# Second block's norm factor applied to the products' results instead of their operand; chunk 0's products placed behind chunk 1's tiles

## The chip, the cores and the metric

One core of one Trainium2 chip runs the kernel. The metric is the device time of one execution in microseconds (us). Engines are named as in the profile: PE (TensorE matmul), PEld (its weight loads), DVE (VectorE), ACT (ScalarE), POOL (GpSimd) and SP (SyncE, which issues the loads).

## The reference, cut to what matters

T = 256 tokens, D = 2048, all in float32. Two blocks run one after the other. The first is an adaLN-modulated neighbourhood attention and a convolutional feed-forward; the second a hybrid layer with an mLSTM and a latent attention, whose input products all come from one normed operand:

```python
def rms_norm_2(x, g):
    x32 = x.astype(jnp.float32)
    y = x32 * lax.rsqrt(jnp.mean(x32 * x32, axis=-1, keepdims=True) + EPS)
    return (y * g.astype(jnp.float32)).astype(x.dtype)
...
    h = rms_norm_2(x, norm_g)
    proj = jnp.einsum('bsd,dn->bsn', h, w_in)
...
    (q_a, k_a, v_a, o_a, i_a, f_a, z_a, c_q, c_kv, k_r, z_b, g_a, g_b) = jnp.split(proj, offsets, axis=-1)
    qk_a = jax.nn.silu(causal_depthwise_conv(jnp.concatenate([q_a, k_a], axis=-1), conv_w))
```

The factor `rsqrt(mean(x*x) + EPS)` is one number per token. It can multiply the operand `h`, or every result of `h @ w_in`, since the product is linear in each token's row. What follows each result differs: `c_q` and `c_kv` are normed again, `k_r` gets its rotation, `i_a` and `f_a` get a bias, `q_a` and `k_a` go through a four-tap convolution along the tokens, `v_a` goes into the mLSTM as it is, and the others pass a sigmoid or silu.

## The kernel before

**Products.** A product is computed in full precision from two parts of each operand: a high part and the rest. A weight tile of 128 x 1024 floats (512 KB) is loaded into one of five buffers `raw`; ACT makes its high part `wh` (L1179), DVE the rest `wl` (L1576), always two tiles ahead of PE (three buffers each). The operand's parts lie in XHL, FHL, HHL and so on. PE does three matmuls per piece: high by high, high by rest, rest by high. Products whose result has tokens in the partitions use L935 to L937 or L926 to L928 (these three with 512 columns); the result lies in PG, a pair of PSUM areas used in turn.

**The order of the work.** `Program` (L156) writes one list of steps by hand: a step is one slice of a product (half a weight tile as a rule), a tile of the adaLN product, or idle. `schedule()` (L258) hangs pieces of other work on steps: `P.put(where, plus, job, key, phase)` places a phase of a job `plus` steps behind a place. Every engine walks the same list and does its own part of each step, in this order: the split of the tile two ahead, the step's matmuls, the side work. So an engine that waits in one piece holds up all that stands behind it on that engine. SP issues the loads in the order of `plan`.

**The start.** The adaLN product comes in eight chunks of eight tiles (L831). While they load, the products for k and v of the first group are done too, two weight tiles per chunk: `early(c)` (L847 to L862), which needs the rows of the shift and scale of chunk c turned into columns (`rows`, L955 and L963 on PE, AR on ACT) and the operand modulated with them (`mod`: MT on DVE, XHL on ACT). In the plan chunk 1 stands as two tiles, two weight tiles, six tiles; the other chunks as eight tiles with the two weight tiles of the chunk before behind them. `early(0)` stands behind the fourth tile of chunk 1, every other behind the eighth tile of its next chunk.

**Attention of the first block.** Heads go in groups of two (g, with hh = 0 and 1). Ten phases of a head stand at steps counted from a place given by hand in `schedule()` (L307 to L312): scores, softmax (SB), its transpose (PT, L1287 on ACT), the product with VB (L1040 on PE) and OHL.

**The border.** The last product of the first block is down1 (four groups). Each group's result is added to the residual XT (`residual`: L1824, L1825, L1828 on DVE). `normed` hangs the second block's norm behind it: ACT squares the last quarter of XT (L1206), DVE makes the factor xr (L1694 to L1604, twelve small operations one after the other), ACT (L1212) and DVE (L1705) multiply XT by it into HNH, PE transposes HNH in eight sets of four (`turned`, L1104; the first three sets ahead of the first product lat 0), and ACT and DVE make the parts of HHL, with the norm's weight g. Behind the last matmul of down1 PE does 28 matmuls whose result nobody reads (`warm`, L1013).

**The second block.** Its products are lat (q and kv latents), small (rotary key and gates), mqk and mv (mLSTM, four groups each, in turn), then sig, silu, out, mix and mixb with others. What follows each: ACT squares of lat (L1352) and LTMP (L1358); small: ACT copies KRF out of PSUM (L1329), DVE adds the biases to the gates (L1895, L1897), PE takes KRF (L1047). Group g of mqk is convolved while mv g is computed (`m_conv`): ACT multiplies the result by the last tap into MQK (L1368, the centre), DVE adds the three others (L1943, three for each of the four quarters, at steps 1 to 4 of mv g) and ACT applies silu. Head 2g + 1 of the mLSTM runs beside mv g + 1: ACT and DVE make ME and MA (L1958) from the gates and scores, DVE multiplies them into MP (L1967), and PE takes MP at L1075.

## Time and profile before

| | |
|---|---|
| median of 3 runs | 2552.49 us (2551.92 to 2555.49) |
| the profiled execution | 2552.33 us, span 2550.3 us, mean granted clock 0.998 |
| PE busy | 2511.5 us, 98% of the span |
| DVE busy | 1619.7 us, 64% |
| ACT busy | 1251.4 us, 49% |
| POOL busy | 143.7 us, 6% |
| DMA | 511.42 MB, 201 GB/s over the span |
| chain that ended last | PE 94%, ACT 2%, DVE 2%, SP's queue 1% |

The span is the time from the first to the last recorded instruction; the execution's own time has about 2 us more around it. A row of a timeline gives the start, the busy time, the engine, the line of the kernel, what is written from what, and in brackets the idle time of the engine before it with what ended it. PEclk is the granted clock of TensorE as a share of full speed (1.00 is 2.4 GHz, 0.50 is 1.2 GHz). Of a busy share, what counts is whether PE, the engine that is hardly ever idle, waits for that engine.

### The profile page before, as it was taken

Reading aid. Unit: us, or ns where it says so; the run is one execution under the profiler, and the core shown is the slowest. Engines: PE = TensorE matmul, PEld = TensorE weight load, DVE = VectorE, ACT = ScalarE, POOL = GpSimd, SP = SyncE. Lnnn points to the kernel's source line nnn. Section 1 sums busy time; section 2 is a strip of 40 time slices with the busy share of each in tenths; the row PEclk is TensorE's granted clock in tenths of the full one; section 3 lists DMA queues with packets and bytes.
Section 4 is the critical chain, followed back from the end, with each engine's and each line's share of the span. In section 5 each row is a group of like instructions: output and inputs, shape, how many; then the busy total and the mean of one; then the engine's idle time right before and its main releaser. Section 6 shows DMA issues by size and latency. Waiting matters only on the chain.

```text
span 2550.3 us, 34507 instructions
## 1 busy us (share of the span) xinstructions
PE 2511.5 (98%) x13608; PEld 2131.9 (84%) x13608; DVE 1619.7 (64%) x2365; ACT 1251.4 (49%) x1899; POOL 143.7 (6%) x148
## 2 busy tenths in 40 slices
...
GB/s 335 333 182 112 233 245 249 244 240 183 206 193 273 266 261 191 193 189 189 191 189 192 163 169 174 174 170 184 174 164 150 157 166 189 181 190 183 189 189 165
DMA packets 459104, 511.42 MB, mean 201 GB/s; under 512 B 36771, under 2 KB 327682, under 8 KB 458432
## 3 DMA queue, kind: packets, MB, share of 16 engines
...
q8 instruction: 107, 1.75, 0.3%
q14 instruction: 53, 0.43, 0.1%
q10 hardware_dynamic: 144, 0.02, 0.0%
...
## 4 chain that ended last, share of the span: by engine, by line
PE 94%; ACT 2%; DVE 2%; SPq 1%; issue 1%; DMA 0%; DVEq 0%; ACTq 0%
PE PG L926 17%; PE PG L928 17%; PE PG L927 17%; PE PG L916 13%; PE PG L919 6%; PE PG L935 4%; PE PG L937 4%; PE PG L936 4%; PE PS L1040 1%; SPq L746 1%; PE PS L831 1%; ACT wh L1179 1%; PE PG L847 1%; PE PS L1104 1%; PE PG L849 1%
## 5 line engine op out<-in xcount | busy, mean ns | idle before, releaser
L1576 DVE TENSOR_TENSOR wl<-raw,wh 128x1024 fp32r<-128x1024 f32 (+1 forms) x745 | 911.3, 1227 | 702.7 <-ACT wh L1179 701.0
L1179 ACT ACTIVATE wh<-raw 128x1024 fp32r<-128x1024 f32 (+1 forms) x745 | 786.7, 1058 | 860.7 <-PE PG L928 574.8
L916 PE MATMUL PG<-FHL,wh 128*128 128x512 f32 x1376 | 430.8, 396 | 2.4 <-DVE UP L1832 1.5
L926 PE MATMUL PG<-wh,HHL 128*128 128x512 f32 x832 | 331.2, 398 | 0.1
L928 PE MATMUL PG<-wl,HHL 128*128 128x512 f32 x832 | 324.8, 390 | 0.0
L927 PE MATMUL PG<-wh,HHL 128*128 128x512 f32 x832 | 324.1, 390 | 0.0
L919 PEld LDWEIGHTS PG<-FHL,wl 128*128 128x128 f32 x1376 | 256.2, 188 | 59.6
L919 PE MATMUL PG<-FHL,wl 128*128 128x256 f32 x1376 | 267.9, 278 | 0.0
L916 PEld LDWEIGHTS PG<-FHL,wh 128*128 128x128 f32 x1376 | 210.8, 189 | 5.2 <-issue 3.7
L928 PEld LDWEIGHTS PG<-wl,HHL 128*128 128x128 f32 x832 | 156.1, 188 | 33.6
L927 PEld LDWEIGHTS PG<-wh,HHL 128*128 128x128 f32 x832 | 156.5, 188 | 30.7
L926 PEld LDWEIGHTS PG<-wh,HHL 128*128 128x128 f32 x832 | 156.3, 188 | 30.6 <-DVE HHL L2069 0.4
L1562 DVE SCALAR_TENSOR_TENSOR ada_acc<-raw,CSs,ada_acc 128x1024 f32<-128x1024 f32 x120 | 161.7, 1347 | 4.7 <-DMA raw<-in_w_ada 0.6
L935 PE MATMUL PG<-XHL,wh 128*128 128x256 f32 (+1 forms) x448 | 150.5, 336 | 0.0
L937 PE MATMUL PG<-XHL,wl 128*128 128x256 f32 (+1 forms) x448 | 147.3, 329 | 0.0
L936 PE MATMUL PG<-XHL,wh 128*128 128x256 f32 (+1 forms) x448 | 147.3, 329 | 0.0
L927 PE MATMUL PG<-wh,HID 128*128 128x512 f32 x344 | 133.8, 389 | 0.0
L926 PE MATMUL PG<-wh,HID 128*128 128x512 f32 x344 | 133.8, 389 | 0.0
L928 PE MATMUL PG<-wl,HID 128*128 128x512 f32 x344 | 133.8, 389 | 0.0
L926 PE MATMUL PG<-wh,XHL 128*128 128x256 f32 x384 | 110.6, 288 | 0.0
L928 PE MATMUL PG<-wl,XHL 128*128 128x256 f32 x384 | 108.6, 283 | 0.0
L927 PE MATMUL PG<-wh,XHL 128*128 128x256 f32 x384 | 108.6, 283 | 0.0
...
## 6 DMA issues: line engine op xcount, KB each, us to landing
...
raw<-in_w_ada SPq DMA_DIRECT2D x128, 512.0 KB, 5.0
...
```

The source lines that it names most:

```text
L746: sp.dma_start(dst[:, :, col:col + wd], src).then_inc(s_raw[P.slot[i]], 16)
L916: pe.matmul(to, hi[:, 128 * j:128 * j + 128], flat(FHL[:, step.k, :, :]), start=step.first, stop=False, skip_group_check=True)
L919: end = pe.matmul(to[:, 0:T], lo[:, 128 * j:128 * j + 128], xh, start=False, stop=step.last, skip_group_check=True)
L926: pe.matmul(dst, xh[:, cols], hi, start=step.first and j % per == 0, stop=False, skip_group_check=True)
L927: pe.matmul(dst, xl[:, cols], hi, start=False, stop=False, skip_group_check=True)
L928: end = pe.matmul(dst, xh[:, cols], lo, start=False, stop=step.last, skip_group_check=True)
L935: pe.matmul(dst, hi[:, c0:c1], xh, start=step.first and j % per == 0, stop=False, skip_group_check=True)
L936: pe.matmul(dst, hi[:, c0:c1], xl, start=False, stop=False, skip_group_check=True)
L937: end = pe.matmul(dst, lo[:, c0:c1], xh, start=False, stop=step.last, skip_group_check=True)
L1179: ac.activation(wh[n % NSPL][:, 0:src.shape[1]], src, ACT.Copy).then_inc(S["hi"], 1)
L1562: dv.scalar_tensor_tensor(out=acc[:, :], in0=raw_of(i), scalar=CSs[:, 0, k:k + 1], in1=acc[:, :], op0=ALU.mult, op1=ALU.add).then_inc(S["a ...
L1576: dv.tensor_tensor(wl[n % NSPL][:, 0:x], src, wh[n % NSPL][:, 0:x], ALU.subtract).then_inc(S["lo"], 1)
```

## The change

It has three parts.

1. *Start.* In the plan every chunk stands as five adaLN tiles, the two weight tiles of the chunk before, three tiles. `early(0)` stands behind all eight tiles of chunk 1, and the rows of chunk 1 are turned at `early(0)` instead of at chunk 1's last tile.
2. *Attention, g = 1.* Phases 6 to 9 of head 2 move from steps 25, 25, 26, 26 to 27, 27, 29, 29, and those of head 3 by up to two steps.
3. *The second block's norm.* XT is transposed as it is: six of the eight sets during down1, two during lat 0. `warm` and the products HNH are gone. The factor is made during lat 0. Where tokens lie in the partitions, ACT multiplies by xr in the operation it does anyway, in two halves instead of one (lat, mv, sig, silu, out, mix, mixb). Where they lie in the columns, the factor is needed as a row: DVE makes DIAGH (identity times xr), PE multiplies it by ones into all partitions (new L1027), ACT copies that to RR. DVE then multiplies small's results by RR and adds the biases after it, and multiplies the whole result of mqk by RR into a new tile MSG, from which centre and taps read. The file's lines move: L926 to L928 are L936 to L938, L1576 is L1598, L1179 is L1195, L1104 is L1120, L1075 is L1089.

```diff
-            tiles, n = chunk_tiles(c), 2 if c == 1 else 8
+            tiles, n = chunk_tiles(c), 5
...
-                if c and n % 8 == (3 if c == 1 else 7):
+                if c and n % 8 == 7:
...
-        at = ("early", c - 1, 0) if c > 1 else ("chunk", 8 * c + 7, 0)
+        at = ("early", c - 1, 0) if c else ("chunk", 8 * c + 7, 0)
...
-            after, plus = ("k", 2, 0), ((14, 15, 16, 17, 18, 19, 25, 25, 26, 26), (27, 27, 28, 28, 29, 30, 32, 32, 33, 34))
+            after, plus = ("k", 2, 0), ((14, 15, 16, 17, 18, 19, 27, 27, 29, 29), (27, 28, 29, 29, 30, 31, 33, 33, 34, 35))
...
     residual("down1", ("tail2", 0, 0), 0, "h")
-    normed("h", ("tail2", 0, 0), ("lat", 0, 0))
+    P.put(("lat", 0, 0), 1, "norm", "h", 0)
+    for phase, n in enumerate((2, 4, 5)):
+        P.put(("lat", 0, 0), n, "rows_h", 0, phase, phase == 1)
+    for i in range(8):
+        turned("xh", i, ("down1", i // 2 + 1, 0) if i < 6 else ("lat", 0, 0), (5 if i < 6 else 3) + 3 * (i % 2))
...
+        P.put(("mv", g, 0), 0, "m_conv", g, 6)
         P.put(("mv", g, 0), 0, "m_conv", g, 0)
...
-             "xf": (HN["f"], FHL[:, :, :, :].rearrange("p k a t -> p a k t"), "f", A1[:, 0, :]), "xh": (HN["h"], HHL, "h", g2)}
+             "xf": (HN["f"], FHL[:, :, :, :].rearrange("p k a t -> p a k t"), "f", A1[:, 0, :]), "xh": (XT, HHL, "h", g2)}
...
-                p = P.of["up" if key == "f" else "lat", 0]
+                p = P.of["up", 0]
                 t = p + 1
...
+            elif (job, phase) == ("rows_h", 1):
+                w.wait_ge(S["diag_h"], 1)
+                w.wait_ge(*free(u))
+                pe.matmul(ps[:, 0:T], ones[:, :], flat(DIAGH[:, :, :]), start=True, stop=True).then_inc(S["side"], 1)
...
-            elif (job, phase) == ("small", 0):
-                w.wait_ge(*product_done("small", 0))
-                ac.activation(KRF[:, :], result("small", 0)[0:64, 0, 0:T], ACT.Copy).then_inc(S["kr_raw"], 1)
+            elif (job, phase) == ("rows_h", 2):
+                u = use("rows_h", 0, 1)
+                w.wait_ge(*full(u))
+                ac.activation(RR[:, :], bank(u)[:, 0:T], ACT.Copy).then_inc(emptying(u), 1)
...
                 w.wait_ge(*product_done("lat", key))
+                w.wait_ge(S["xr"], 2)
                 if key == 1:
                     w.wait_ge(S["lat_r"], 1)
                 for n in range(2):
-                    end = ac.activation(LJUNK[:, n, :], result("lat", key)[:, n, :], ACT.Square,
+                    end = ac.activation(LJUNK[:, n, :], result("lat", key)[:, n, :], ACT.Square, scale=xr[:, n:n + 1],
...
                 g, b = key, key % 2
-                w.wait_ge(*product_done("mqk", g))
+                w.wait_ge(*out_done("mqk", g))
                 if g >= 2:
                     w.wait_ge(*full(use("mlstm", 2 * g - 3, 0, 1)))
                 for j in range(4):
                     ch = 8 * (j // 2) + 2 * g + j % 2
-                    end = ac.activation(MQK[b][:, j, :], result("mqk", g)[:, j // 2, T * (j % 2):T * (j % 2) + T],
-                                        ACT.Identity, scale=cw2[:, 3, ch:ch + 1])
+                    end = ac.activation(MQK[b][:, j, :], MSG[b][:, j, :], ACT.Identity, scale=cw2[:, 3, ch:ch + 1])
                 end.then_inc(S["m_centre"], 1)
...
-                ac.activation(RG[n % 2][:, :, :], result(name, g)[:, :, :],
-                              ACT.Sigmoid if name == "sig" else ACT.Silu).then_inc(out_sem(name, g), 1)
+                for j in range(2):
+                    end = ac.activation(RG[n % 2][:, j, :], result(name, g)[:, j, :],
+                                        ACT.Sigmoid if name == "sig" else ACT.Silu, scale=xr[:, j:j + 1])
...
                 ps = result("small", 0)
-                dv.tensor_scalar(gates[:, 0, :], ps[64:72, 0, 0:T], gb[:, 0:1], None, ALU.add)
-                w.wait_ge(S["kr_raw"], 1)
-                dv.tensor_scalar(gates[:, 1, :], ps[96:104, 0, 0:T], gb[:, 1:2], None,
-                                 ALU.add).then_inc(out_sem("small", 0), 1)
+                w.wait_ge(*product_done("small", 0))
+                w.wait_ge(*emptied(use("rows_h", 0, 1)))
+                dv.tensor_tensor(KRF[:, :], ps[0:64, 0, 0:T], RR[0:64, :], ALU.mult).then_inc(S["kr_raw"], 1)
+                dv.tensor_tensor(gates[:, 0, :], ps[64:72, 0, 0:T], RR[64:72, :], ALU.mult)
+                dv.tensor_tensor(gates[:, 1, :], ps[96:104, 0, 0:T], RR[96:104, :], ALU.mult).then_inc(c.sem, c.up())
+                w.wait_ge(c.sem, c.n)
+                dv.tensor_scalar(gates[:, 0, :], gates[:, 0, :], gb[:, 0:1], None, ALU.add)
+                dv.tensor_scalar(gates[:, 1, :], gates[:, 1, :], gb[:, 1:2], None, ALU.add).then_inc(out_sem("small", 0), 1)
+            elif (job, phase) == ("rows_h", 0):
+                w.wait_ge(S["xr"], 2)
+                dv.tensor_tensor(DIAGH[:, :, :], ident[:, :].unsqueeze(1).to_broadcast([128, 2, 128]),
+                                 xr[:, :].unsqueeze(2).to_broadcast([128, 2, 128]), ALU.mult).then_inc(S["diag_h"], 1)
+            elif (job, phase) == ("m_conv", 6):
+                g, b = key, key % 2
+                w.wait_ge(*product_done("mqk", g))
+                w.wait_ge(*emptied(use("rows_h", 0, 1)))
+                if g >= 2:
+                    w.wait_ge(S["m_centre"], g - 1)
+                dv.tensor_tensor(MSG[b][:, :, :], result("mqk", g)[:, :, :].rearrange("p a (c n) -> p (a c) n", c=2),
+                                 RR[:, :].unsqueeze(1).to_broadcast([128, 4, T]), ALU.mult).then_inc(out_sem("mqk", g), 1)
...
-                dv.tensor_copy(lr[:, 2 * key:2 * key + 2], y).then_inc(S["lat_r"], 1)
+                dv.tensor_tensor(lr[:, 2 * key:2 * key + 2], y, xr[:, :], ALU.mult).then_inc(S["lat_r"], 1)
...
                 w.wait_ge(S["m_centre"], g + 1)
+                w.wait_ge(*out_done("mqk", g))
                 for k in (2, 1, 0):
                     d = 3 - k
                     end = dv.scalar_tensor_tensor(
-                        out=MQK[b][:, j, d:T], in0=result("mqk", g)[:, j // 2, T * (j % 2):T * (j % 2) + T - d],
+                        out=MQK[b][:, j, d:T], in0=MSG[b][:, j, 0:T - d],
                         scalar=cw2[:, k, ch:ch + 1], in1=MQK[b][:, j, d:T], op0=ALU.mult, op1=ALU.add)
```

How DVE's order changes at mv 1, with head 1 beside it. wl is a weight tile's rest, MQK the convolution's sum, MA and MP belong to the head. Before:

```order
L1576 TENSOR_TENSOR wl_65<-raw_53,wh_62 128x1024
L1943 SCALAR_TENSOR_TENSOR MQK_187<-PG,cw_101,MQK_187 128x255
L1943 SCALAR_TENSOR_TENSOR MQK_187<-PG,cw_101,MQK_187 128x254
L1943 SCALAR_TENSOR_TENSOR MQK_187<-PG,cw_101,MQK_187 128x253
L1576 TENSOR_TENSOR wl_66<-raw_49,wh_63 128x1024
L1958 TENSOR_TENSOR MA<-PS,caus_k 128x256
L1943 SCALAR_TENSOR_TENSOR MQK_187<-PG,cw_101,MQK_187 128x255
```

Now:

```order
L1598 TENSOR_TENSOR wl_65<-raw_53,wh_62 128x1024
L1935 TENSOR_TENSOR MSG_217<-PG,RR 128x1024
L1982 SCALAR_TENSOR_TENSOR MQK_187<-MSG_217,cw_101,MQK_187 128x255
L1982 SCALAR_TENSOR_TENSOR MQK_187<-MSG_217,cw_101,MQK_187 128x254
L1982 SCALAR_TENSOR_TENSOR MQK_187<-MSG_217,cw_101,MQK_187 128x253
L1598 TENSOR_TENSOR wl_66<-raw_49,wh_63 128x1024
L1997 TENSOR_TENSOR MA<-PS,caus_k 128x256
L1982 SCALAR_TENSOR_TENSOR MQK_187<-MSG_217,cw_101,MQK_187 128x255
```

MSG has come in between the split of the third tile of mv 1 and the first tap; the rest is in its old order.

PE at the border, from the last matmuls of down1 (HID is its operand) to the first of lat 0 (HHL). Before:

```order
L927 MATMUL PG<-wh_62,HID 128x512
L928 MATMUL PG<-wl_65,HID 128x512
L1013 MATMUL PG<-wh_63 128x512 x28
L1104 MATMUL PS<-ident,HNH 128x128 x12
L926 MATMUL PG<-wh_63,HHL 128x512
L927 MATMUL PG<-wh_63,HHL 128x512
L928 MATMUL PG<-wl_66,HHL 128x512
```

Now, from the last piece of lat 0's second tile on; the two tiles ahead of it follow down1 with nothing between:

```order
L937 MATMUL PG<-wh_64,HHL 128x512
L938 MATMUL PG<-wl_67,HHL 128x512
L1120 MATMUL PS<-ident,XT 128x128 x4
L936 MATMUL PG<-wh_62,HHL 128x512
L937 MATMUL PG<-wh_62,HHL 128x512
L938 MATMUL PG<-wl_65,HHL 128x512
L936 MATMUL PG<-wh_62,HHL 128x512
L937 MATMUL PG<-wh_62,HHL 128x512
L938 MATMUL PG<-wl_65,HHL 128x512
L1027 MATMUL PS<-DIAGH,ones 128x256
L936 MATMUL PG<-wh_62,HHL 128x512
```

The filler and the twelve transposes that stood ahead of lat 0 are gone; one set of four transposes stands behind its second tile, and the matmul on DIAGH in the middle of its third.

DVE's order there, from the last residual of down1 to the second block's first operand parts. Now:

```order
L1847 TENSOR_TENSOR RTMP<-PG,G_166 128x512
L1850 TENSOR_TENSOR XT<-RTMP,XT 128x512 x2
L1598 TENSOR_TENSOR wl_65<-raw_51,wh_62 128x1024
L1716 SCALAR_TENSOR_TENSOR xss<-xsq,xss 128x2
...
L1626 SCALAR_TENSOR_TENSOR xr<-CV 128x2
L1598 TENSOR_TENSOR wl_66<-raw_52,wh_63 128x1024
L1927 TENSOR_TENSOR DIAGH<-ident,xr 128x256
L1598 TENSOR_TENSOR wl_67<-raw_53,wh_64 128x1024
L2120 SCALAR_TENSOR_TENSOR HHL<-PS,g_91,HHL 128x256 x2
```

Before, the norm followed the residual with no split between, and the split of the third tile stood behind six sets of transposes:

```order
L1825 TENSOR_TENSOR RTMP<-PG,G_166 128x512
L1828 TENSOR_TENSOR XT<-RTMP,XT 128x512 x2
L1694 SCALAR_TENSOR_TENSOR xss<-xsq,xss 128x2
...
L1604 SCALAR_TENSOR_TENSOR xr<-CV 128x2
L1705 TENSOR_SCALAR HNH<-XT,xr 128x256 x3
L2069 SCALAR_TENSOR_TENSOR HHL<-PS,g_91,HHL 128x256 x2
...
L1705 TENSOR_SCALAR HNH<-XT,xr 128x256
L1576 TENSOR_TENSOR wl_65<-raw_51,wh_62 128x1024
```

The split of lat 0's third tile has moved ahead of the norm chain, and DIAGH stands behind the chain and one more split.

## Rows read from the trace of the kernel before

**Rows 1.** The page, section 1: busy time and instructions of each engine.
```profile
PE 2511.5 (98%) x13608; PEld 2131.9 (84%) x13608; DVE 1619.7 (64%) x2365; ACT 1251.4 (49%) x1899; POOL 143.7 (6%) x148
```

**Rows 2.** Table by stage: stretch, its length, busy us (instructions) by engine, clock, DMA.
```profile
42.00:53.00 11.00, 11.00 (x48) 8.96 (x48) 0.00 (x0) 1.79 (x3) 0.00 (x0) 0.98 1.10 348
...
63.10:66.00 2.90, 2.84 (x7) 2.27 (x8) 1.14 (x2) 0.18 (x1) 0.00 (x0) 0.50 1.10 351
...
269.00:272.00 3.00, 0.54 (x5) 0.37 (x4) 2.05 (x3) 2.72 (x5) 0.00 (x0) 1.00 0.02 10
```

**Rows 3.** Timeline of PE, start: start us, us, engine, line, operands, [idle before].
```profile
39.94 1.92 PE L831 MATMUL PS<-raw,CSP 128*32 128x512 f32 x4
...
53.20 1.92 PE L831 MATMUL PS<-raw,CSP 128*32 128x512 f32 x16
...
63.16 0.80 PE L847 MATMUL PG<-XHL,wh 128*128 128x512 f32 x1 [2.67 <-DVE wl L1576]
...
76.66 0.64 PE L831 MATMUL PS<-raw,CSP 128*32 128x512 f32 x4
```

**Rows 4.** Timeline of ACT, start.
```profile
74.02 1.06 ACT L1179 ACTIVATE wh<-first 128x1024 fp32r<-128x1024 f32 x1 [1.52 <-DMA first<-in_w_qkv]
```

**Rows 5.** Timelines of ACT and PE, head work of g = 1.
```profile
270.76 1.07 ACT L1287 ACTIVATE PT<-PS 128x512 f32<-128x512 f32 x2
...
271.92 1.32 PE L1040 MATMUL PS<-PT,VB 128*128 128x256 f32 x5 [2.46 <-ACT PT L1287]
```

**Rows 6.** Timeline of PE, border between the two blocks.
```profile
1443.40 6.51 PE L1013 MATMUL PG<-wh 128*128 128x512 f32 x28
1450.75 1.53 PE L1104 MATMUL PS<-ident,HNH 128*128 128x128 f32 x12 [0.84 <-ACT HNH L1212]
1452.42 0.50 PE L926 MATMUL PG<-wh,HHL 128*128 128x512 f32 x1
```

**Rows 7.** Timelines of DVE and ACT, border between the two blocks.
```profile
1445.73 1.28 DVE L1828 TENSOR_TENSOR XT<-RTMP,XT 128x512 f32<-128x512 f32 x2
1447.82 0.16 DVE L1694 SCALAR_TENSOR_TENSOR xss<-xsq,xss 128x2 f32<-128x2 f32 x1 [0.80 <-ACT HNH L1206]
...
1450.19 1.31 ACT L1212 ACTIVATE HNH<-XT,xr 128x256 f32<-128x256 f32 x3 [2.40 <-DVE xr L1604]
```

**Rows 8.** Timeline of DVE, mv 1 with head 1 beside it.
```profile
1580.68 1.23 DVE L1576 TENSOR_TENSOR wl<-raw,wh 128x1024 fp32r<-128x1024 f32 x1 [1.66 <-ACT wh L1179]
1582.14 1.52 DVE L1943 SCALAR_TENSOR_TENSOR MQK<-PG,cw,MQK 128x255 f32<-128x255 f32 x3 [0.23 <-ACT MQK L1368]
1583.69 1.22 DVE L1576 TENSOR_TENSOR wl<-raw,wh 128x1024 fp32r<-128x1024 f32 x1
1584.83 0.42 DVE L1958 TENSOR_TENSOR MA<-PS,caus_k 128x256 f32<-128x256 f32 x1
...
1589.40 0.55 DVE L1967 SCALAR_TENSOR_TENSOR MP<-PS,ME 128x384 f32<-128x384 f32 x1
```

**Rows 9.** Timeline of PE, mv 1, where PE takes MP.
```profile
1590.01 0.70 PE L1075 MATMUL PS<-MV,MP 128*128 128x257 f32 x2
```

**Rows 10.** Groups of DVE instructions by line: busy us, mean ns, idle before.
```profile
L1716 DVE SCALAR_TENSOR_TENSOR MT<-X,A,RX 128x256 f32<-128x256 f32 x16 | 7.7, 482 | 0.9
...
L1943 DVE SCALAR_TENSOR_TENSOR MQK<-PG,cw,MQK 128x254 f32<-128x254 f32 x16 | 7.7, 481 | 0.6
...
L2021 DVE TENSOR_TENSOR QKT<-PG,CV 128x1024 f32<-128x1024 f32 x8 | 9.8, 1224 | 0.3
```

**Rows 11.** Timelines of DVE and PE, mv 0.
```profile
1540.73 1.22 DVE L1576 TENSOR_TENSOR wl<-raw,wh 128x1024 fp32r<-128x1024 f32 x1
...
1543.04 0.39 PE L926 MATMUL PG<-wh,HHL 128*128 128x512 f32 x1
```

**Rows 12.** Timelines of DVE and PE, small product.
```profile
1509.15 0.48 DVE L1895 TENSOR_SCALAR gates<-PG,gb 8x256 f32<-8x256 f32 x1
...
1508.96 0.33 PE L1047 MATMUL PS<-ident,KRF 64*128 64x64 f32 x2
```

More of the change, by code:

```diff
@@ L583, in build @@
     RT = at("RT", [128, 2, 4, 64], F32, 199)
+    DIAGH = at("DIAGH", [128, 2, 128], F32, 178)
+    RR = at("RR", [128, T], F32, 179)
+    MSG = [at(f"MSG{i}", [128, 4, T], F32, 140 + 4 * i) for i in range(2)]
     KRH = at("KRH", [128, 2, 4, 64], F32, 201)
@@ L608, in xready @@
         u = use("turned", ("x" + z, k // 2), 0)
-        return emptied(u + k) if k < 2 else emptied(u)
+        return emptied(u + k) if z == "f" and k < 2 else emptied(u)
     def bank(u):
@@ L1095, in piece @@
                 w.wait_ge(*free(u))
-                apart = name in ("xf", "xh") and i == 0
+                apart = name == "xf" and i == 0
                 for ch in range(2):
@@ L1377, in piece @@
                     w.wait_ge(*full(use("mlstm", 2 * key - 3, 4, 1)))
-                ac.activation(MV[key % 2][:, :, :, 0:T], result("mv", key)[:, :, :].rearrange("p j (h e) -> p j h e", h=2),
-                              ACT.Copy).then_inc(out_sem("mv", key), 1)
+                for n in range(2):
+                    end = ac.activation(MV[key % 2][:, n, :, 0:T], result("mv", key)[:, n, :].rearrange("p (h e) -> p h e", h=2),
+                                        ACT.Copy, scale=xr[:, n:n + 1])
+                end.then_inc(out_sem("mv", key), 1)
             elif (job, phase) == ("mlstm", 2):
@@ L1415, in piece @@
                     w.wait_ge(*full(use("turned", ("ha", 7), 0)))
-                ac.activation(cols4(GA if name == "mix" else GB, g), result(name, g)[:, :, :],
-                              ACT.Sigmoid).then_inc(out_sem(name, g), 1)
+                for j in range(2):
+                    end = ac.activation(cols4(GA if name == "mix" else GB, g)[:, j, :], result(name, g)[:, j, :],
+                                        ACT.Sigmoid, scale=xr[:, j:j + 1])
+                end.then_inc(out_sem(name, g), 1)
             elif (job, phase) == ("qr_out", 0):
@@ L1506, in piece @@
                 w.wait_ge(*full(u))
-                if name in ("xf", "xh") and i == 0:
-                    if name == "xf":
-                        w.wait_ge(S["gain"], NCH + 1)
+                if name == "xf" and i == 0:
+                    w.wait_ge(S["gain"], NCH + 1)
                     for k in range(2):
```

33 lines of the change are left out of this document (16 added, 17 removed).

## The prediction

> **What bounds the kernel now.** The page's first section was read first: PE is busy 2511.5 of 2550.3 us, DVE 64% and ACT 49% [rows 1]. So only PE's own instructions and its waits count; a change on DVE or ACT counts where PE waits for it. The table by stage then places the waits. The stretches of the start show DMA at a share of 1.10, PE at half clock (0.50) in 63.1 to 66, and a wait at 269 to 272 with the clock at 1.00 [rows 2]. Last came the timelines of PE, DVE and ACT at the places the change touches: the start [rows 3, 4], 271.92 [rows 5], the border between the blocks [rows 6, 7], the mLSTM heads [rows 8 to 10] and the small product [rows 12]. After 76 us no wait of PE is longer than 2.5 us. A gain must therefore come from PE instructions removed or from one of these few waits, and a delay costs only what exceeds the slack PE has there. About 0.2% (5.1 us) is what a measurement of this kernel can tell from no change.
>
> **Start (load plan, chunk 0's products behind chunk 1's tiles).** Loads set the pace. The 14th load is used at 39.94 [rows 3] and the 37th at 74.02 [rows 4], so one takes 34.08 / 23 = 1.48 us. The first 18 loads are the same set in another order, and chunk 1's last tile is the 18th: it lands at 39.94 + 4 x 1.48 = 45.9. Chunk 0's products began right behind the tiles of 39.94 (1.92 us) and ended at 53.20, 11.4 us later [rows 3]; now they begin near 47 and end near 59 (11.4 of their own, 0.8 for the L963 group that follows chunk 1's tiles). In return the 1.9 us of tiles that stood behind them at 53.20 are done before, and the 2.67 us wait at 63.16 for the weights of chunk 1's products should go, because those weights and chunk 1's modulated rows are made while chunk 0's products still run. Chunk 2's eight tiles (3.6, at 1.92 for four, less the overlap) then end near 63. Chunk 1's products took 63.16 to 76.66, 13.5 us, of which about 1.4 was half clock; without that they end near 75.2. That is 1.4 us earlier. Against it, PE does only short tile work with gaps before 47, and may begin chunk 0's products at half clock as it did at 63.16, which would return up to 1.4. I take **+1.0 us gained** (ends: -0.5 and +2.2). Once ahead, PE gives the next chunk's loads a little less time, but a chunk takes 3.6 + 12.0 = 15.6 us on PE at full clock and its ten loads 14.8, so 0.8 us is left each time.
>
> **Places of head work for g = 1.** The wait of 2.46 us at 271.92 is for ACT's PT copies, 270.76 to 271.8, which ACT does behind an operand split [rows 5]. PE's step moves from 26 to 29, about three steps later, so this wait goes. But ACT now has the VB eviction ahead of PT (128x1024 like a split's, so some 1.0 us, [rows 4]), and DVE and ACT have the next head's copies behind it, so two waits of about 1 us are what is late next. I take **+0.6** (ends -1 and +2.5).
>
> **Border between the blocks.** Before, from the last product of the first block at 1443.40 to the first of the second at 1452.42, PE does 28 filler matmuls (6.51), waits 0.84 and does 12 transposes (1.53) [rows 6]. Five later sets of four transposes add 0.35 each, so 9.02 + 1.75 = 10.8 us in all. Now eight sets of four (2.8) and one 128x256 matmul (0.45) remain: 7.5 us less. Two new waits take part of it. XT is final at 1447.0 (DVE L1828, from 1445.73), ACT's squares of it are done at 1447.8, where DVE's chain begins at 1447.82 [rows 7]. The second block's third weight tile is split behind these: ACT to 1448.8, DVE to 1450.0. PE, which starts at 1443.40 and spends 2.73 us on a tile, wants it at 1443.40 + 5.45 + 0.35 = 1449.2: a wait of 0.8. Behind that split stand the norm chain (2.4 us, 1447.82 to 1450.19 before), the fourth tile's split (1.2) and DIAGH (0.42), so DIAGH is ready at about 1453.9, while PE reaches its matmul at 1451.4: a wait of 2.5. Net 7.5 - 3.3 = **+4.2** (ends: +7.5 with no new wait, +2.5 if the clock falls after the second one).
>
> **mLSTM heads 1, 3, 5.** This is the term that decides. In mv 1 to mv 3, DVE has no idle time between the first tap at 1582.14 and MP, which ends at 1589.95; PE takes MP at 1590.01, with the sequencer there just in time [rows 8, 9]. The change puts MSG (128x1024 out of PSUM) into DVE's order between the wl split at 1580.68 and the first tap, and makes ACT's centre wait for it, where it ran beside that split before. An instruction follows a wl split after 1.14 us (1583.69 to 1584.83), so MSG starts at 1581.82; a 128x1024 multiply out of PSUM takes 1.22 [rows 10]; the centre starts at 1583.1. It reads SBUF now: four at the 0.40 us spacing of L1212 [rows 7] end at 1584.8. The taps start at 1584.85 instead of 1582.14, **2.7 us later**, and everything behind them is as before: wl, MA, six taps, wl, MP. Three times 2.7 = 8.1 us lost. In mv 0 there is no head, but the fifth tile's split, 1540.73 to 1541.95, moves by 2.7 to 1544.65, and PE wants it at 1543.04 [rows 11]: 1.6 more. **-9.7 in all.** The lower bound is zero only if PE had slack at 1590.01, which the rows exclude; 2.3 each (a centre as fast as from PSUM, a tap shorter) gives -8; a fall of the clock after such a wait adds 1.4 each.
>
> The taps read SBUF now. Rows show no gain in that: a tap out of PSUM takes 481 ns, the same operation all out of SBUF 482 [rows 10]. The Trainium skill (VectorE: DVE Perf Modes, "Rules for kernel authors" and the table of its section on the TRN2 errata) speaks for the copy: it advises moving a matmul result to SBUF before many operations on it, and its table has 62 cycles less for a source in SBUF. By that, an estimate from the page, each of nine taps would be 65 ns shorter and each of the three waits 0.6 us shorter; the row on L1716 does not bear it out.
>
> **Small product.** KRF is no longer an ACT copy but DVE's, behind two splits, where the first gate operation stood at 1509.15; it ends at 1509.6 and PE, which took it at 1508.96, waits 0.65 [rows 12]. Three more DVE operations follow, but ACT's gate chain starts late by the same 0.65, so the later wait near 1520 keeps its size. **-0.7** (ends 0 and -2).
>
> **Edits at about nothing.** HNH's scalings leave DVE and ACT at the border, where they were already counted. Evictions in two halves add about 0.25 us each on ACT; between them and the next PE wait ACT has idle time in the head stages, else they would cost up to 0.5 in all. I take -0.1. SP's loads are otherwise in the old order.
>
> **Sum:** 1.0 + 0.6 + 4.2 - 9.7 - 0.7 - 0.1 = -4.7, so 2552.3 (the profiled execution; the median of the runs, 2552.5, is 0.2 above it) becomes 2557.0, and as a median **2557.2 us**.
>
> **Rivals.** (1) *The clock falls after the new waits.* Four waits of 2.5 to 2.7 us are new. After the 2.67 us at 63.16 the next 2.9 us went at half clock, after the 2.46 us at 271.92 they did not [rows 2, 5]: the rows allow both. At two of four it costs 1.4 x 2 = 2.8, so 2560; at all four 2563. The filler matmuls that the change removes kept PE busy at the border. The Trainium skill (TensorE: Matmul & The Clock Gate, "Why this matters for your kernels") warns of idle gaps between bursts of matmuls, since they bring the array back to the low clock. Chance 0.25. (2) *The mLSTM stages absorb MSG.* If MP or its consumer had about 2.7 us of slack, the sum turns to +5.0 and with the border's gain whole to +8: 2544 to 2547. For it: DVE is only 64% busy. Against: the row at 1590.01 comes 0.06 after MP's end. It decides from about 0.5 us of slack per stage upward, and a full turn to faster needs all. Chance 0.12. (3) *The parts cancel.* The centre and taps cost 2.2 instead of 2.7, the border loses only one wait and the start gives its upper end: -6.6 - 1.1 (mv 0) + 6.5 + 2 + 0.6 - 0.8 = +0.6, so 2551.7; between this and the forecast lies 2552 to 2555. Chance 0.2. My forecast has 0.43.
>
> **Numbers.** The forecast's own spread, 2555 to 2559, straddles the border of 2557.6, so it gives half of its 0.43 to slower and half to no change. With rival 1 slower gets 0.21 + 0.25, rival 3 gives 0.2 to no change, rival 2 0.12 to faster. Slower 0.46, same 0.42, faster 0.12. The range leaves out rival 2 and rival 1 at all four places with more beside it: 2549 to 2564.
>
> **What the profile after would show.** Right: three waits of 2.3 to 2.7 us at the first PE instruction that takes MP (L1089 in the new file), a wait near 1.5 in mv 0 for a wl split, one near 2.5 for DIAGH at the new L1027 and one below 1 for wl before it; no filler matmuls at the second border; chunk 1's products beginning right behind chunk 2's tiles. Wrong: no wait for MP, which would mean that DVE was not the one on whom PE waited; PEclk under 1.00 behind the waits (rival 1); or chunk 0's products starting after 49.

## The result and the profile after

The changed kernel takes 2562.41 us (median of 6 runs, 2561.57 to 2563.57) where before takes 2552.41 (6 runs): **10.0 us slower**, ratio 1.0037 with a 95% interval of 1.0027 to 1.0048. The forecast was 2557.2 with a range of 2549 to 2564: right in its sign and its range, but 4.7 us of loss were forecast and 10.0 came, so half of the size.

The page of the kernel after, sections 1 and 4, beside [rows 1]:

```profile
span 2561.2 us, 34472 instructions
...
PE 2512.7 (98%) x13582; PEld 2129.4 (83%) x13582; DVE 1623.5 (63%) x2365; ACT 1253.0 (49%) x1915; POOL 143.4 (6%) x148
...
PE 92%; DVE 3%; ACT 2%; SPq 1%; issue 1%; DMA 1%; DVEq 0%; ACTq 0%
```

PE is busy 2512.7 us, 1.2 more than before although the filler is gone, and the span grew by 10.9 us: the rest is new waiting. DVE's share of the chain went from 2% to 3%. Now PE's waits of the kernel after (line waited at, who ended the wait, us in total, times, the longest):

```profile
...
PE PS L1089 <- DVE MP L2006: 7.6, 3, 2.6
PE PS L841 <- DMA raw<-in_w_ada: 3.2, 1, 3.2
PE PS L841 <- DMA first<-in_w_ada: 2.8, 3, 1.9
PE PS L1159 <- ACT LS L1503: 2.3, 3, 0.8
PE PS L1027 <- DVE DIAGH L1927: 2.2, 1, 2.2
PE PG L936 <- DVE wl L1598: 1.8, 2, 1.2
...
PE PS L1166 <- ACT LP L1510: 1.0, 3, 0.3
...
PE PS L1061 <- DVE KRF L1919: 0.5, 1, 0.5
```

L1089 takes MP (L1075 before), L1027 is the matmul on DIAGH, L936 waits for weight tiles' wl (in lat 0 and in mv 0), L1166 for LP in the latent attention. The waits at L1089, L1027, L936, L1166 and L1061 were not there before; the one at L1159 was 1.7 us in all.

Where the time went, by the start of the same matmul in the two traces:

| stretch | PE against before | forecast |
|---|---|---|
| start, up to 76 us | -1.8 | -1.0 |
| attention, g = 1 | -0.5 | -0.6 |
| 428 us (L993 waits for SQ) | +0.7 | none |
| border, down1 to the middle of lat 0 | -2.4 | -4.2 |
| small product (KRF) | +0.7 | +0.7 |
| mv 0 (wl) | +1.5 | +1.6 |
| mv 1, 2, 3: three waits for MP | +8.3 | +8.1 |
| half clock behind two of these three | +2.9 | none (rival 1) |
| latent attention (L1166) | +1.5 | +0.1 |
| sum | +10.9 | +4.7 |

The rows of the mLSTM stage, DVE in mv 1, the same instructions as in [rows 8]:

```profile
1579.04 1.23 DVE L1598 TENSOR_TENSOR wl<-raw,wh 128x1024 fp32r<-128x1024 f32 x1 [1.65 <-ACT wh L1195]
1580.19 1.22 DVE L1935 TENSOR_TENSOR MSG<-PG,RR 128x1024 f32<-128x1024 f32 x1
1583.18 1.52 DVE L1982 SCALAR_TENSOR_TENSOR MQK<-MSG,cw,MQK 128x255 f32<-128x255 f32 x3 [1.78 <-ACT MQK L1386]
1584.73 1.23 DVE L1598 TENSOR_TENSOR wl<-raw,wh 128x1024 fp32r<-128x1024 f32 x1
1585.88 0.42 DVE L1997 TENSOR_TENSOR MA<-PS,caus_k 128x256 f32<-128x256 f32 x1
...
1590.46 0.55 DVE L2006 SCALAR_TENSOR_TENSOR MP<-PS,ME 128x384 f32<-128x384 f32 x1
```

ACT's centre, four instructions, and PE's first use of MP:

```profile
1581.44 1.71 ACT L1386 ACTIVATE MQK<-MSG,cw 128x256 f32<-128x256 f32 x4 [2.43 <-DVE MSG L1935]
```

```profile
1591.06 0.70 PE L1089 MATMUL PS<-MV,MP 128*128 128x257 f32 x2 [2.54 <-DVE MP L2006]
```

MSG starts 1.15 us behind the wl split and ends at 1581.4; only then ACT starts the centre (it had 2.43 us idle, the releaser is MSG), and DVE idles 1.78 us until 1583.18. From there to MP the distance is 7.28 us, as before (1582.14 to 1589.40, 7.26). PE waits 2.54 us.

Table by stage of the kernel after (stretch, length, busy us of PE, PEld, DVE, ACT, POOL, clock, DMA share, GB/s): the start, and each of four waits with the 3 us behind it. For the first wait for MP one more stretch shows the clock's lower level by itself.

```profile
47.00:53.00 6.00, 6.00 (x32) 4.96 (x31) 1.77 (x9) 1.44 (x3) 0.00 (x0) 1.00 1.09 358
...
1452.60:1455.10 2.50, 0.38 (x2) 0.00 (x0) 2.33 (x8) 0.03 (x1) 0.00 (x0) 1.00 0.61 193
1455.20:1458.20 3.00, 3.00 (x9) 2.36 (x10) 1.83 (x3) 0.39 (x1) 0.00 (x0) 0.60 0.67 200
1588.50:1591.00 2.50, 0.02 (x1) 0.00 (x0) 2.43 (x5) 1.96 (x2) 0.00 (x0) 1.00 0.13 45
1591.00:1594.20 3.20, 3.14 (x10) 2.64 (x11) 2.63 (x7) 1.52 (x4) 0.00 (x0) 0.71 0.53 164
1592.40:1595.60 3.20, 3.20 (x10) 2.46 (x9) 1.30 (x4) 2.05 (x6) 0.00 (x0) 0.50 0.61 182
1642.60:1645.10 2.50, 0.00 (x0) 0.00 (x0) 2.43 (x5) 1.92 (x2) 0.00 (x0) 1.00 0.12 40
1645.10:1648.10 3.00, 2.97 (x13) 2.55 (x14) 2.60 (x6) 1.36 (x3) 0.00 (x0) 1.00 0.57 175
1695.00:1697.50 2.50, 0.01 (x1) 0.00 (x0) 2.43 (x5) 1.97 (x2) 0.00 (x0) 1.00 0.11 43
1697.50:1700.60 3.10, 3.03 (x8) 2.45 (x9) 2.64 (x7) 1.41 (x3) 0.00 (x0) 0.60 0.54 169
```

The clock has two levels here, 1.00 and 0.50; a value between is the mean of a stretch that holds both. Behind the wait of 2.19 us for DIAGH the mean was 0.60, behind the first and the third wait for MP 0.71 and 0.60, so it fell to 0.50 for a part of each; behind the second it stayed at 1.00, though the three were of the same length. The start shows a part at the lower level only ahead of chunk 0's products, which ran at 1.00.

PE at the start and at the border:

```profile
47.12 0.50 PE L857 MATMUL PG<-XHL,wh 128*128 128x512 f32 x1
...
62.77 0.50 PE L857 MATMUL PG<-XHL,wh 128*128 128x512 f32 x1
...
1450.12 0.60 PE L1120 MATMUL PS<-ident,XT 128*128 128x128 f32 x4
1451.33 0.50 PE L936 MATMUL PG<-wh,HHL 128*128 128x512 f32 x1 [0.60 <-DVE wl L1598]
...
1455.16 0.70 PE L1027 MATMUL PS<-DIAGH,ones 128*128 128x256 f32 x2 [2.19 <-DVE DIAGH L1927]
```

Chunk 0's products begin at 47.12 (forecast: near 47) and chunk 1's at 62.77 with no wait. At the border the third tile waits 0.60 us for wl (forecast 0.8) and the DIAGH matmul 2.19 (forecast 2.5).

### The profile page after: what moved, and what is told of

It reads as the page before. It is cut to its first block, busy times and chain, and to the rows that moved or that the text cites. A ratio compares the mean times of both kernels' runs of the same rounds, so it can differ in the third digit from the quotient of the medians.

```text
span 2561.2 us, 34472 instructions
## 1 busy us (share of the span) xinstructions
PE 2512.7 (98%) x13582; PEld 2129.4 (83%) x13582; DVE 1623.5 (63%) x2365; ACT 1253.0 (49%) x1915; POOL 143.4 (6%) x148
## 4 chain that ended last, share of the span: by engine, by line
PE 92%; DVE 3%; ACT 2%; SPq 1%; issue 1%; DMA 1%; DVEq 0%; ACTq 0%
PE PG L936 17%; PE PG L938 17%; PE PG L937 17%; PE PG L926 13%; PE PG L929 6%; PE PG L945 4%; PE PG L947 4%; PE PG L946 4%; SPq L756 1%; PE PS L1054 1%; PE PS L841 1%; ACT wh L1195 1%; DVE wl L1598 1%; DVE MQK L1982 1%; PE PG L857 1%
## 5 line engine op out<-in xcount | busy, mean ns | idle before, releaser
L1598 DVE TENSOR_TENSOR wl<-raw,wh 128x1024 fp32r<-128x1024 f32 (+1 forms) x745 | 911.5, 1227 | 710.8 <-ACT wh L1195 708.8
L1195 ACT ACTIVATE wh<-raw 128x1024 fp32r<-128x1024 f32 (+1 forms) x745 | 785.2, 1057 | 851.3 <-PE PG L938 563.5
L926 PE MATMUL PG<-FHL,wh 128*128 128x512 f32 x1376 | 430.8, 396 | 2.4 <-DVE UP L1854 1.5
L936 PE MATMUL PG<-wh,HHL 128*128 128x512 f32 x832 | 333.3, 401 | 1.8 <-DVE wl L1598 1.8
L938 PE MATMUL PG<-wl,HHL 128*128 128x512 f32 x832 | 326.0, 392 | 0.0
L926 PEld LDWEIGHTS PG<-FHL,wh 128*128 128x128 f32 x1376 | 210.8, 189 | 5.2 <-issue 3.7
L936 PEld LDWEIGHTS PG<-wh,HHL 128*128 128x128 f32 x832 | 157.4, 189 | 33.8 <-DVE wl L1598 2.9
L938 PEld LDWEIGHTS PG<-wl,HHL 128*128 128x128 f32 x832 | 157.1, 189 | 33.9
L936 PE MATMUL PG<-wh,HID 128*128 128x512 f32 x344 | 134.4, 391 | 0.0
L938 PE MATMUL PG<-wl,HID 128*128 128x512 f32 x344 | 133.9, 389 | 0.0
L936 PE MATMUL PG<-wh,XHL 128*128 128x256 f32 x384 | 110.3, 287 | 0.0
L938 PE MATMUL PG<-wl,XHL 128*128 128x256 f32 x384 | 108.7, 283 | 0.0
```

Source lines behind the costliest of these rows:

```text
L926: pe.matmul(to, hi[:, 128 * j:128 * j + 128], flat(FHL[:, step.k, :, :]), start=step.first, stop=False, skip_group_check=True)
L936: pe.matmul(dst, xh[:, cols], hi, start=step.first and j % per == 0, stop=False, skip_group_check=True)
L938: end = pe.matmul(dst, xh[:, cols], lo, start=False, stop=step.last, skip_group_check=True)
L1195: ac.activation(wh[n % NSPL][:, 0:src.shape[1]], src, ACT.Copy).then_inc(S["hi"], 1)
L1598: dv.tensor_tensor(wl[n % NSPL][:, 0:x], src, wh[n % NSPL][:, 0:x], ALU.subtract).then_inc(S["lo"], 1)
```

## Experiments

**1. The first two parts alone (ab).** Before, with these edits:

```diff
-            tiles, n = chunk_tiles(c), 2 if c == 1 else 8
+            tiles, n = chunk_tiles(c), 5
...
-                if c and n % 8 == (3 if c == 1 else 7):
+                if c and n % 8 == 7:
...
-        at = ("early", c - 1, 0) if c > 1 else ("chunk", 8 * c + 7, 0)
+        at = ("early", c - 1, 0) if c else ("chunk", 8 * c + 7, 0)
...
-            after, plus = ("k", 2, 0), ((14, 15, 16, 17, 18, 19, 25, 25, 26, 26), (27, 27, 28, 28, 29, 30, 32, 32, 33, 34))
+            after, plus = ("k", 2, 0), ((14, 15, 16, 17, 18, 19, 27, 27, 29, 29), (27, 28, 29, 29, 30, 31, 33, 33, 34, 35))
```

> Before with the first two parts of the change alone (start, attention of g = 1). If parts add up, it is 1.8 (start, as the changed kernel's PE rows stand ahead of before's at 76 us) plus 0 to 0.5 (attention) faster than before: 2550.2 to 2550.7 us. If the start's gain came from something else in the changed kernel, or is given back where PE meets the loads, it is within 0.3 us of before, 2552.4.

Measured 2551.18 us where before had 2553.57 timed along with it: ratio 0.9989 (0.9980 to 0.9998), 2.4 us faster by the medians. In the trace PE stands 1.0 us ahead of before at 66 us and 1.5 ahead behind the heads of g = 1. The changed kernel stood 1.8 ahead at 66 us. The difference is the clock under chunk 1's last tiles: in 43 to 47 us its mean was 0.50 here and 0.61 there, in 47 to 49 us 0.74 here and 1.00 there, and chunk 0's products began at 48.02 instead of 47.12. So these two parts bring about what was forecast (1.6) and it is not given back.

**2. The norm's part alone (c_alone).** The changed kernel with the same edits undone.

> The changed kernel with the first two parts undone, so the norm's part alone. If parts add up, the gain of 2.3 us that these two had alone is missing: 2562.4 + 2.3 = 2564.7 us where before is 2552.4, 12.3 above before. If they hang together, it is elsewhere by more than 1 us.

Measured 2564.44 against 2552.71: ratio 1.0042 (1.0028 to 1.0057), 11.7 us slower. With the 2.4 of experiment 1 that makes 9.3, against 10.0 measured for the whole: the parts add up within 1 us. The wait of 2.7 us at the start and the one of 2.5 for PT are back in its list of waits. Here the clock fell behind DIAGH and the second and third wait for MP, and not behind the first. It also fell behind the wait for PT (0.50 in 273.3 to 276.3 us), behind which it had stayed at 1.00 before.

**3. MSG left out (no_msg).** The piece of DVE is gone, centre and taps read PSUM again (shown without the semaphores that change with it). The kernel leaves out the factor per token in q and k of the mLSTM:

```diff
-        P.put(("mv", g, 0), 0, "m_conv", g, 6)
...
-                    end = ac.activation(MQK[b][:, j, :], MSG[b][:, j, :], ACT.Identity, scale=cw2[:, 3, ch:ch + 1])
+                    end = ac.activation(MQK[b][:, j, :], result("mqk", g)[:, j // 2, T * (j % 2):T * (j % 2) + T],
+                                        ACT.Identity, scale=cw2[:, 3, ch:ch + 1])
...
-                        out=MQK[b][:, j, d:T], in0=MSG[b][:, j, 0:T - d],
+                        out=MQK[b][:, j, d:T], in0=result("mqk", g)[:, j // 2, T * (j % 2):T * (j % 2) + T - d],
```

> The changed kernel with MSG left out: centre and taps read mqk's results out of PSUM as before, so q and k of the mLSTM lack the factor per token. My theory, MSG's place in DVE's order holds up MP by 2.7 us: the three waits for MP (7.6 us) and the wait for wl in mv 0 (1.2 us) go, with two falls of the clock behind them (2.9 us), so about 2562.4 - 11.7 = 2550.7 us. Rival, MP is late because its inputs from ACT are late: the waits stay over 1.5 us each and the time is over 2557 us.

Measured 2549.50 against 2553.57: 0.9984 (0.9975 to 0.9994). That is 12.9 us below the changed kernel (14.1 when each is set against the before timed along with it), 1.2 more than expected, and no wait for MP is left in its list. The rival, inputs late from ACT, falls with them. One instruction of 1.22 us, four times in the program, cost 13 us together with what waited for it. The matmul on DIAGH and the 3 us behind it in this trace:

```profile
1456.15 0.70 PE L1026 MATMUL PS<-DIAGH,ones 128*128 128x256 f32 x2 [2.18 <-DVE DIAGH L1927]
...
1456.20:1459.20 3.00, 3.00 (x13) 2.50 (x14) 1.81 (x3) 1.26 (x2) 0.00 (x0) 1.00 0.76 195
```

The wait is the changed kernel's, but this time the clock stayed at 1.00 behind it. In its other executions this is not known.

**4. Taps spread over the stage (taps_spread).**

```diff
-            P.put(("mv", g, 0), 1 + j, "m_conv", g, 1 + j)
-        P.put(("mv", g, 0), 6, "m_conv", g, 5)
+            P.put(("mv", g, 0), 2 + 2 * j, "m_conv", g, 1 + j)
+        P.put(("mv", g, 0), 10, "m_conv", g, 5)
```

> The changed kernel with the convolution's taps at steps 2, 4, 6 and 8 of mv instead of 1 to 4, and silu at step 10 instead of 6. MSG stays. My theory, DVE has enough time in the stage and only its order delays MP: the three waits for MP shrink below 0.3 us each, mv 0's wait goes, the clock stays up: 2550 to 2552 us. Rival, DVE's amount of work in mv is what is short: a wait of about 1.2 us each, for MP or for a weight tile's wl, comes back at another step: 2556 us or more.

Measured 2563.15 against 2553.57: 1.0036 (1.0023 to 1.0049), no gain at all. The theory fell as it had been put. PE's waits in it:

```profile
PE PG L936 <- DVE wl L1598: 6.7, 4, 2.2
...
PE PS L1089 <- DVE MP L2006: 2.9, 3, 1.0
```

The waits for MP shrank from 2.5 to 1.0 us each, but three waits for wl of about 2 us came in some 12 us later, and the clock fell behind two of them. The rival expected that from a lack of DVE time. ACT's timeline tells it differently (mv 1 starts at 1576.0 here):

```profile
1579.74 1.71 ACT L1386 ACTIVATE MQK<-MSG,cw 128x256 f32<-128x256 f32 x4 [2.43 <-DVE MSG L1935]
1581.36 1.04 ACT L1195 ACTIVATE wh<-raw 128x1024 fp32r<-128x1024 f32 x1
...
1592.13 0.38 ACT L1413 ACTIVATE MSQ<-PS 128x256 f32<-128x256 f32 x1 [5.26 <-DVE dcol L2013]
...
1592.87 2.00 ACT L1195 ACTIVATE wh<-raw 128x1024 fp32r<-128x1024 f32 x2
```

The centre sits in front of the next tile's high part: ACT idles 2.43 us for MSG, and wh comes 2.3 us late in the stage, then wl, MA, ME and MP with it. Later MSQ waits 5.26 us for sums that DVE makes behind the third tap, and the next two wh wait behind MSQ. DVE had idle time in all of this. These rows speak for the order on *two* engines and not the amount on one; experiment 5 tests it.

**5. The order on both engines (best1).** On top of the changed kernel:

```diff
-        P.put(("mv", g, 0), 0, "m_conv", g, 0)
+        P.put(("mv", g, 0), 2, "m_conv", g, 0)
...
-            P.put(("mv", g, 0), 1 + j, "m_conv", g, 1 + j)
-        P.put(("mv", g, 0), 6, "m_conv", g, 5)
+            P.put(("mv", g, 0), (3, 5, 8, 11)[j], "m_conv", g, 1 + j)
+        P.put(("mv", g, 0), 13, "m_conv", g, 5)
...
-    for phase, n in enumerate((2, 4, 5)):
+    for phase, n in enumerate((2, 8, 9)):
...
-                P.put(at, n, "square", (norm, g), 0)
+                P.put(*((("lat", 0, 0), 0) if norm == "h" and g == 3 else (at, n)), "square", (norm, g), 0)
```

> The changed kernel with three moves in its step table: the convolution's centre at step 2 of mv, behind the next tile's high part on ACT, taps at 3, 5, 8 and 11, silu at 13; DIAGH's matmul at step 8; the last squares of XT behind the split of lat 0's third tile. My theory after the first four runs: it is not DVE's amount of work but what MSG, centre and taps stand ahead of on each engine (wh and MA, then MP, then the head's sums). So no wait for MP or wl over 0.5 us in mv 0 to mv 3, clock at 1.00, none for DIAGH: 2562.4 - 12.9 (MSG, from the run without it) - 3.8 - 0.9 = about 2545 us. Rival, mv has too little DVE time: waits of 1 us or more per stage stay and it is over 2549 us.

Measured **2546.03 us** (2544.98 to 2546.32) against 2553.41: ratio 0.9970 (0.9958 to 0.9982). It is 7.4 us faster than before and 16.4 faster than the changed kernel. DVE, ACT and PE in mv 1:

```profile
1572.81 1.22 DVE L1935 TENSOR_TENSOR MSG<-PG,RR 128x1024 f32<-128x1024 f32 x1
1574.41 1.22 DVE L1598 TENSOR_TENSOR wl<-raw,wh 128x1024 fp32r<-128x1024 f32 x1 [0.38 <-ACT wh L1195]
1575.56 0.42 DVE L1997 TENSOR_TENSOR MA<-PS,caus_k 128x256 f32<-128x256 f32 x1
1576.01 1.52 DVE L1982 SCALAR_TENSOR_TENSOR MQK<-MSG,cw,MQK 128x255 f32<-128x255 f32 x3
...
1579.47 0.55 DVE L2006 SCALAR_TENSOR_TENSOR MP<-PS,ME 128x384 f32<-128x384 f32 x1
...
1573.32 1.06 ACT L1195 ACTIVATE wh<-raw 128x1024 fp32r<-128x1024 f32 x1 [1.69 <-PE PG L938]
1574.29 1.69 ACT L1386 ACTIVATE MQK<-MSG,cw 128x256 f32<-128x256 f32 x4
...
1580.99 0.59 PE L1089 MATMUL PS<-MV,MP 128*128 128x257 f32 x2
```

MSG, of the same length in the same place, is hidden: wh of the next tile stands ahead of the centre now, MA is done before the first tap, MP ends at 1580.02 and PE takes it at 1580.99 with no wait. Its list has no wait for MP, for DIAGH, or for wl in lat 0 and mv, so the rival, too little DVE time, is refuted. The three moves were made together; what the one of DIAGH is worth alone is experiment 6, the other two were not separated.

**6. DIAGH's matmul four steps later (rows_later).** The change of `(2, 4, 5)` to `(2, 8, 9)` of experiment 5 alone.

> The changed kernel with the matmul on DIAGH and the copy to RR four steps later (steps 8 and 9 of lat 0 instead of 4 and 5). If DIAGH was simply not ready, its wait (2.2 us) and the half clock behind it (1.6 us) go and nothing takes their place: 2562.4 - 3.8 = 2558.6 us. If the wait moves on to the next thing behind the norm chain on DVE, the fourth tile's wl, at least 1 us of it comes back and the time is over 2559.5 us.

Measured 2559.78 against 2553.41: 1.0024 (1.0014 to 1.0033), 6.4 above before where the changed kernel was 10.0 above: 3.6 gained, where 3.8 was expected. The median by itself is 2.6 below the changed kernel's and over the 2559.5 at which the rival was set, but the median of before, timed along with it, was 1.0 higher too, so the times alone don't exclude it. In the trace PE gains 2.7 us at the old place of DIAGH's matmul and 0.6 net behind it, where the changed kernel ran at half clock. A wait of 0.48 us for the fourth tile's wl took the wait's place, the one that the rival names, at half of the size it needed. The three waits for MP are as long as before (2.54 to 2.56), and the clock fell behind the second alone.

**7. Matmuls in the wait (fill_wait).** In front of the wait for MP of heads 1, 3 and 5:

```diff
+                    if h in (1, 3, 5):
+                        w.wait_ge(*free(u))
+                        for _ in range(5):
+                            pe.matmul(ps[:, 0:T], ident[:, :], GROW[:, :], start=True, stop=True)
                     w.wait_ge(*emptied(use("mlstm", h, 0, 1)))
```

> The changed kernel with five more matmuls (128x256, identity by GROW, about 0.45 us each, their result overwritten) ahead of each of the three waits for MP, 2.3 us of work inside 2.5 us of waiting. If the clock falls because PE idles there, it stays at 1.00 behind all three and the 2.9 us of half clock at two of them go: about 2559.5 us. If it falls for another reason, or the fillers delay PE, the time is 2562.4 us or more.

Measured 2559.14 against 2553.57: 5.6 above before instead of 10.0 (1.0025, 1.0015 to 1.0035). Its stretches, the first wait with what is behind it, and what is behind the third:

```profile
1588.50:1591.00 2.50, 2.11 (x11) 1.53 (x10) 2.43 (x5) 1.31 (x2) 0.00 (x0) 1.00 0.01 2
1591.00:1594.20 3.20, 3.20 (x16) 2.66 (x15) 2.02 (x5) 2.17 (x6) 0.00 (x0) 1.00 0.63 171
...
1695.50:1698.60 3.10, 3.10 (x15) 2.60 (x16) 2.41 (x6) 1.66 (x4) 0.00 (x0) 1.00 0.55 169
```

The clock is 1.00 behind the waits, where its mean was 0.71 and 0.60. MP comes when it came before, and the time is 3.3 us shorter by the medians, 4.4 when each is set against the before timed along with it (the traces show 1.5 behind the first and 1.5 behind the third). So the fall goes with PE's idle time. It is well supported and not proved: without these matmuls the clock fell behind 5 of 9 such waits for MP (2 of 3 in the changed kernel, 2 of 3 in experiment 2, 1 of 3 in experiment 6), so three spared in one trace could be luck with a chance of about one in eleven (an estimate from the 5 of 9). But all nine executions timed here (2558.66 to 2560.96) lie below all six of the changed kernel.

**8. The old filler taken out (no_filler).** Before, with the 28 matmuls at the second border left out.

> Before, with the 28 filler matmuls at the second border left out and nothing else (PE waits there 7.3 us for HNH). If the filler is what keeps the clock up, the granted clock is 0.50 for about 3 us behind the wait and the time is 1.4 us above before's. If the clock doesn't depend on it, the time is the same within 0.3 us.

By the medians 1.5 us slower (2554.88 against 2553.41), by the ratio not to be told from before (1.0003, 0.9994 to 1.0013). The trace shows more. Its stretches at the border:

```profile
1443.00:1450.00 7.00, 0.11 (x1) 0.00 (x0) 5.78 (x18) 1.60 (x5) 0.00 (x0) 0.66 0.43 143
1450.00:1453.00 3.00, 2.70 (x13) 2.70 (x14) 1.79 (x6) 3.00 (x8) 0.00 (x0) 0.50 0.00 0
...
1456.00:1459.00 3.00, 3.00 (x16) 2.43 (x16) 2.35 (x5) 2.30 (x4) 0.00 (x0) 1.00 0.34 81
```

The clock fell within a wait of 7.2 us, was 0.50 behind it and back at 1.00 by 1456, and PE lost 2.0 us from the first transpose to the fourth set (it stood 0.45 us ahead of before there and 1.56 behind it afterwards). So the filler was worth some 1 to 2 us, and the 6.5 us of it cost nothing, because PE would have waited that long. What the change saves at the border is that wait, not the filler.

**9. The gate evictions whole (rg_whole).** best1 with the edit below, which leaves out the factor per token in these gates:

```diff
-                for j in range(2):
-                    end = ac.activation(RG[n % 2][:, j, :], result(name, g)[:, j, :],
-                                        ACT.Sigmoid if name == "sig" else ACT.Silu, scale=xr[:, j:j + 1])
-                end.then_inc(out_sem(name, g), 1)
+                ac.activation(RG[n % 2][:, :, :], result(name, g)[:, :, :],
+                              ACT.Sigmoid if name == "sig" else ACT.Silu).then_inc(out_sem(name, g), 1)
```

> best1 with the 12 gate evictions (sig, silu, out) whole again and without the factor per token, so these gates are wrong by that factor. If halving them costs PE 0.5 us at each of three waits for LP, the time is 1.5 us below best1: 2544.5 us where before is 2553.4. If halving is hidden, as the prediction had it, the time is best1's within 0.3 us.

Measured 2545.02 against 2552.71, a ratio of 0.9966 (0.9954 to 0.9979) where best1 had 0.9970: the times can't tell. The traces can: at 1572 us this execution stood 1.6 us behind best1 for waits of the first block that differ from one execution to the next; from there it gains six times 0.25 us, twice in each of three groups of heads (at LS and at LP), and ends 0.1 behind. The waits for LP are gone. By these two traces halving costs 1.5 us.

**10. Evictions later (best2), heads later (best3).** Two attempts to hide that. best2 is best1 with

```diff
-            P.put(nxt, 0, "gate", x, 0)
-            P.put(nxt, 1, "gate", x, 1)
+            P.put(nxt, 3, "gate", x, 0)
+            P.put(nxt, 4, "gate", x, 1)
```

> As best1, and the gate evictions (RG on ACT and its product on DVE) at steps 3 and 4 of the next product instead of 0 and 1. If the 0.5 us more at the three waits for LP come from the halved evictions ahead of it on ACT, these waits go: 1.5 to 2 us less than best1. If they now stand ahead of another head's work, the time is as best1's or above.

2559.46 against 2553.41, 13 us worse than best1. The waits for LP are gone, but

```profile
PE PG L936 <- ACT RG L1429: 9.9, 6, 2.8
```

the next product but one starts before the eviction has freed its PSUM area, where the products are short. best3 moves heads 1 and 3 of each group of four by one step instead:

```diff
-                    P.side[base + step * hh + n].append(("mla", 4 * g + hh, phase, uses))
+                    P.side[base + step * hh + n + (g < 3 and hh % 2)].append(("mla", 4 * g + hh, phase, uses))
```

> best1 with two of four heads of the latent attention (hh = 1 and 3, g = 0 to 2) one step later, so that their LS no longer stands right behind qr's small copies and their LP no longer behind the gate eviction on ACT. The three waits for LS (0.75 us each) and the three for LP (0.33 us each, 0.5 with what they add to before) shrink: up to 3.5 us below best1. If ACT's amount of work in these short products is what is short, the waits move to the neighbouring heads: within 0.5 us of best1.

2545.22 us (2544.41 to 2546.41) against 2552.71, 0.9967 (0.9954 to 0.9980). The waits for LP are gone from its list, those for LS grew to 2.6 us in all. Its ratio is best1's within the interval, as the second branch has it: the waits moved to neighbours. Both beat before and the changed kernel; which of them is better can't be told.

## Why the prediction was right and where not

- **The deciding term, the mLSTM heads, was right in place, mechanism and size.** It said 2.7 us at each of three places and 1.6 in mv 0. Measured 2.8, 2.8, 2.7 and 1.5 by the offsets of PE's rows, and experiment 3 shows that they come with MSG and go with it. What it didn't look at is that the centre, once it waits for MSG, also keeps back the next wh on ACT. Here DVE came later still, so this cost nothing, but it is why moving the taps alone did not help (experiment 4).
- **What was missing from the sum is the clock**, put as a rival with a chance of 0.25. "At two of four it costs 1.4 x 2 = 2.8, so 2560; at all four 2563" is near what came: three of four places, 1.6 + 1.5 + 1.4 = 4.5 us, which is most of the 5 us missed, and the prediction's own sign of being wrong, a clock under 1.00 behind the waits, was there. The rows of before had one wait of each kind, 2.67 us with the fall and 2.46 without. One of two would have put half of 4 x 1.4 us, so 2.8, into the sum, and the forecast at 2560. The Trainium skill (TensorE: Matmul & The Clock Gate, "Why this matters for your kernels") warns of idle gaps of PE between bursts of matmuls. It has longer gaps in mind than those of 2.19 to 2.56 us that were followed by the fall here; the measurement decides. Which of two equal waits is followed by it, no run here foretells: over the profiled executions of the changed kernel and its variants it was 9 of 14 waits for DIAGH and MP.
- **Halved evictions: -0.1 forecast, -1.5 measured** (experiment 9). "Between them and the next PE wait ACT has idle time in the head stages" did not hold in the latent attention, where short products follow each other: waits for LP of 1.0 us came in and those for LS grew by 0.6.
- **Border: +4.2 forecast, +2.4 measured.** The waits were 0.6 and 2.2 instead of 0.8 and 2.5. A set of four transposes costs 0.46 us, not 0.35, since the matmul behind it starts late too (1452.42 had shown 0.50 where 0.39 is usual); this falls on before as well. The rest is mainly the 1.6 us of half clock; about 0.4 us (an estimate from these terms) is not assigned; a part may be PE's slower start behind each of the two waits, where the first matmul took 0.50 again.
- **Start: +1.0 forecast, +1.8 measured**, 1.0 in experiment 1's execution. The half clock that was feared for chunk 0's products did not come in 47 to 53 us; it fell on the tiles ahead of them, and in experiment 1's execution it lasted longer there. The 0.8 us more that the start gave hid a part of what the clock and the evictions cost, and that was luck. Attention (+0.6, measured 0.5) was right. Small (-0.7, 0.7) was right in its sum, the wait for KRF itself was 0.47 where 0.65 was forecast. The wait near 1520 nearly kept its size (0.83, 1.01 before).
- **A small slip in rival 3:** a border that loses only the wait of 0.8 us is 7.5 - 0.8 = 6.7, not 6.5. It changes neither its time by more than 0.2 us nor its chance.
- **The taps did not get shorter out of SBUF.** Groups by line of the kernel after:

```profile
L1935 DVE TENSOR_TENSOR MSG<-PG,RR 128x1024 f32<-128x1024 f32 x4 | 4.9, 1217 | 0.0
...
L1982 DVE SCALAR_TENSOR_TENSOR MQK<-MSG,cw,MQK 128x254 f32<-128x254 f32 x16 | 7.7, 483 | 0.6
...
L1429 ACT ACTIVATE RG<-PG,xr 128x512 f32<-128x512 f32 x24 | 15.2, 684 | 0.1
```

  483 ns against 481 out of PSUM [rows 10]. The estimate from the Trainium skill (VectorE: DVE Perf Modes, the table of its section on the TRN2 errata), 65 ns less per tap, is not borne out here; the measurement decides.
- **Open:** 0.7 us at 428 us, where L993 waited 0.41 us for SQ. No part of the change touches this place. The lists of best2 and best3 have such a wait too (0.2 and 0.6), those of experiments 1 to 7 have not, so it may differ from one execution to the next. It has no experiment of its own.
